# A hybrid decoder trunk on one core: adding the expert results during the last job, and level scores issued within a projection

## What is computed

```python
# HGRN2, per chunk: scores with a decay per feature
b = jnp.cumsum(gb, axis=2)
decay = jnp.exp(where(mask, b[:, :, :, None, :] - b[:, :, None, :, :], -inf))
scores = jnp.einsum('bhtd,bhsd,bhtsd->bhts', qb, kb, decay)
# experts: each token goes to its two best of 8, weighted by a softmax over the two
top_val, top_idx = lax.top_k(logits, TOP_K)
gates = jax.nn.softmax(top_val, axis=-1)
hid = jax.nn.silu(xb @ w_gate[e]) * (xb @ w_up[e])
ys = (hid @ w_down[e]) * gt[:, None]          # for the tokens of expert e
y = zeros.at[tok_pad].add(ys)                 # each token's two results are added
x = x + y
return rmsnorm(x, final_norm)
```

## Time and profile before

| | us |
|---|---|
| median of 3 runs | 1554.12 |
| lowest, highest | 1554.05, 1557.11 |
| the profiled execution, its own time | 1557.37 |
| its span, first to last instruction | 1555.6 |
| mean granted TensorE clock in it | 0.971 |

### The profile page before, as it was taken

One profiled execution on the slowest core, in us unless ns is written; L12 is line 12 of the kernel. 1 busy time (PEld: TensorE's weight loads), 2 busy tenths in 40 slices (PEclk: granted clock), 3 DMA queues, 4 the chain that ended last, 5 costly groups with the idle time before them and its releaser, 6 DMA issues.

```text
span 1555.6 us, 21085 instructions
## 1 busy us (share of the span) xinstructions
PE 1477.0 (95%) x8033; PEld 1257.2 (81%) x8033; DVE 1165.6 (75%) x921; ACT 952.6 (61%) x847; POOL 90.9 (6%) x103
## 2 busy tenths in 40 slices
PE   6999799997999979999999999999999999999993
PEld 6988499997988658888888888888888888888882
DVE  4883354544686258888888888888888888889884
ACT  4454244443545227777777777777777777777772
POOL 4221000000031120000000000000000000000001
PEclk8999999999899969999999999999999999999997
DMA  8431695543333169999999999999999999999983
GB/s 262 163 109 55 210 317 190 190 138 133 109 113 112 49 229 349 388 376 375 396 367 374 395 387 370 395 369 370 394 379 366 394 387 373 394 370 365 395 339 108
DMA packets 211785, 449.19 MB, mean 289 GB/s; under 512 B 12884, under 2 KB 37016, under 8 KB 211736
## 3 DMA queue, kind: packets, MB, share of 16 engines
q1 hardware_dynamic: 210584, 444.31, 78.5%
q0 software_dynamic: 1152, 4.19, 0.7%
HBM read 433.80 MB, written 14.68 MB: 288 GB/s over the span
## 4 chain that ended last, share of the span: by engine, by line
PE 89%; DVE 5%; ACT 2%; issue 1%; DMA 1%; SPq 1%; POOL 0%; DVEq 0%; POOLq 0%; ACTq 0%
PE bank L1371 26%; PE bank L1373 26%; PE bank L1372 26%; PE bank L1594 2%; PE bank L1581 2%; PE bank L1678 2%; ACT winh L711 1%; PE bank L1425 1%; DVE QD L995 1%; DVE low L1223 1%; DMA ring<-in_w_in_dram 1%; DVE winl L963 1%; DVE SC L1004 0%; ACT XN L679 0%; PE bank L1665 0%
## 5 line engine op out<-in xcount | busy, mean ns | idle before, releaser
L1223 DVE TENSOR_TENSOR low<-raw,high 128x2048 fp32r<-128x2048 f32 x336 | 769.1, 2298 | 112.2 <-ACT high L880 112.2
L880 ACT CAST high<-raw 128x2048 fp32r<-128x2048 f32 x336 | 644.6, 1919 | 178.0 <-PE bank L1373 178.0
L1371 PE MATMUL bank<-high,xeh 128*128 128x512 f32 x896 | 353.5, 395 | 0.0
L1373 PE MATMUL bank<-high,xel 128*128 128x512 f32 x896 | 349.5, 390 | 0.0
L1372 PE MATMUL bank<-low,xeh 128*128 128x512 f32 x896 | 348.8, 389 | 0.0
L1373 PEld LDWEIGHTS bank<-high,xel 128*128 128x128 f32 x896 | 168.2, 188 | 35.8
L1372 PEld LDWEIGHTS bank<-low,xeh 128*128 128x128 f32 x896 | 168.4, 188 | 33.7
L1371 PEld LDWEIGHTS bank<-high,xeh 128*128 128x128 f32 x896 | 168.3, 188 | 33.7 <-issue 0.2
L1371 PE MATMUL bank<-high,hdh 128*128 128x512 f32 x448 | 175.0, 391 | 0.0
L1373 PE MATMUL bank<-high,hdl 128*128 128x512 f32 x448 | 174.4, 389 | 0.0
L1372 PE MATMUL bank<-low,hdh 128*128 128x512 f32 x448 | 174.3, 389 | 0.0
(11 more groups left out here) (281 smaller groups left out, 1945.0 us busy)
## 6 DMA issues: line engine op xcount, KB each, us to landing
raw<-in_moe_w_gate_dram SPq DMA_DIRECT2D x112, 1024.0 KB, 7.7
raw<-in_moe_w_up_dram SPq DMA_DIRECT2D x112, 1024.0 KB, 8.2
raw<-in_moe_w_down_dram SPq DMA_DIRECT2D x112, 1024.0 KB, 7.7
ring<-in_w_in_dram SPq DMA_DIRECT2D x10, 2048.0 KB
dring<-in_dense_w_gate_dram SPq DMA_DIRECT2D x5, 2048.0 KB
dring<-in_dense_w_up_dram SPq DMA_DIRECT2D x5, 2048.0 KB
dring<-in_dense_w_down_dram SPq DMA_DIRECT2D x5, 2048.0 KB
ring<-in_w_in_dram SPq DMA_DIRECT2D x8, 1024.0 KB
```

The costliest lines, as they stand in the source:

```text
L880: act.copy(high[:, q % SPLIT, :], raw[:, q % RAW, :]).then_inc(s_hi, 1)
L1223: dve.tensor_tensor(low[:, q % SPLIT, :], raw[:, q % RAW, :], high[:, q % SPLIT, :].bitcast(F32), ALU.subtract).then_inc(s_lo, 1)
L1371: pe.matmul(o, xh, wh, start=first, stop=False)
L1373: return pe.matmul(o, xl, wh, start=False, stop=last)
```

## The change

In the layers, level k-1 is issued between the two groups of projection k+2, where level k stood behind projection k+2.

At the end:
- GpSimd prepares, behind the scatters of the tokens, selection matrices for the last job (picks: row = token, column = slot in the last job, value = the weight of that choice) and row numbers in which all places of the last job point to a block of `routed` that holds zeros (pick_last).
- At piece 16 of the last job (BACK_AT) VectorE converts these row numbers, and GpSimd gathers the results of all other jobs into a buffer of their own, multiplies each by its weight and adds it to X, while the last job runs.
- Behind the last job ScalarE and VectorE copy its results, TensorE turns the selection matrices (ScalarE copies them) and multiplies them with the results: four fp32 products of 128x128 by 128x512. VectorE adds these to X.
- Squares, scaling and stores go by halves of 512 features; mean and power by tiles.
- The last store to `routed` and the wait for it are gone.

```diff
+    BACK_AT = STORE_AT + 3
-        gathered = raw[:, :, :].rearrange("p r n -> p (r n)")[:, 0:2 * T * D]....
+        gathered = phase("experts", "gathered", [P, 2, T, D])
...
@@ SP
-            sp.wait_ge(s_yh, 2 * njobs + 2)
-            sp.dma_start(routed[bass.ds(njobs, 1), :, :]..., results[:, :]).then_inc(s_last, 16)
...
             for t in range(T):
-                sp.wait_ge(s_fin, t + 1)
-                sp.dma_start(out[0, t * P:(t + 1) * P, :], XN[:, t, :]).then_inc(s_out, 16)
+                for n in range(2):
+                    v = slice(n * BANK, (n + 1) * BANK)
+                    sp.wait_ge(s_fin, 2 * t + n + 1)
+                    sp.dma_start(out[0, t * P:(t + 1) * P, v], XN[:, t, v]).then_inc(s_out, 16)
@@ GpSimd
+            def pick_last():
+                first, rel, past, off = lastb[:, 0:1], lastr[:, 0, :, :], lastr[:, 1, :, :], lastr[:, 2, :, :]
+                step(pool.tensor_scalar(first, JB[:, 1, 15:16], float(P), None, ALU.mult))
+                step(pool.tensor_scalar(rel, places[:, :, :], first, None, ALU.subtract))
+                step(pool.tensor_scalar(past, rel, 0.0, None, ALU.is_ge))
+                step(pool.tensor_scalar(off, places[:, :, :], -1.0, float(P * (MAXJOBS + 1)), ALU.mult, ALU.add))
+                step(pool.tensor_tensor(off, off, past, ALU.mult))
+                step(pool.tensor_tensor(lastr[:, 3, :, :], off, places[:, :, :], ALU.add))
+                for t in range(T):
+                    for c in range(2):
+                        ins = pool.tensor_scalar(picks[:, c, t, :], iota[:, :], rel[:, c, t:t + 1], RV[:, 5 + c, t:t + 1],
+                                                 ALU.is_equal, ALU.mult)
+                step(ins)
+                for t in range(T):
+                    ins = pool.tensor_tensor(picks[:, 0, t, :], picks[:, 0, t, :], picks[:, 1, t, :], ALU.add)
+                ins.then_inc(s_pick, 1)
...
-            pool.wait_ge(s_last, 16)
+            pick_last()
+            pool.wait_ge(s_backi, 1)
             for t in range(T):
                 for c in range(2):
                     pool.indirect_dma_start(gathered[:, c, t, :], None, routed....,
-                                            bass.IndirectOffsetOnAxis(ap=placei[:, c, t:t + 1], axis=0))\
+                                            bass.IndirectOffsetOnAxis(ap=backi[:, c, t:t + 1], axis=0))\
                         .then_inc(s_back[t], 16)
-            inv_rms(2 * DEPTH)
+            for t in range(T):
+                pool.wait_ge(s_back[t], 32)
+                for c in range(2):
+                    g = gathered[:, c, t, :]
+                    pool.tensor_scalar(g, g, RV[:, 5 + c, t:t + 1], None, ALU.mult).then_inc(s_lb3, 1)
+                    pool.wait_ge(s_lb3, 2 * t + c + 1)
+                    if c:
+                        pool.wait_ge(s_ca, 2 * t + 1)
+                    pool.tensor_tensor(X[:, t, :], X[:, t, :], g, ALU.add).then_inc(s_ca, 1)
+            for t in range(T):
+                pool.wait_ge(s_ss, 2 * T * DEPTH + 2 * t + 2)
+                mean = st[:, 2 * DEPTH, 0, t:t + 1]
+                pool.tensor_scalar(mean, mean, fsq[:, t:t + 1], None, ALU.add).then_inc(s_fr, 1)
+                pool.wait_ge(s_fr, 3 * t + 1)
+                pool.tensor_scalar(mean, mean, 1.0 / D, EPS, ALU.mult, ALU.add).then_inc(s_fr, 1)
+                pool.wait_ge(s_fr, 3 * t + 2)
+                pool.tensor_tensor(st[:, 2 * DEPTH, 1, t:t + 1], mean, mhalf[:, 0:1], ALU.pow).then_inc(s_fr, 1)
@@ ScalarE
+            act.wait_ge(s_pickT, 1)
+            act.copy(pickT[:, :, :], ps[6][:, 0:T * P].rearrange("p (t s) -> p t s", t=T)).then_inc(s_pickc, 1)
             act.wait_ge(s_used, nth_use(last, NPC - 1))
-            for n in range(2):
-                results_out(last + 1, n)
+            act.copy(results[:, BANK:], ps[5][:, :]).then_inc(s_lres1, 1)
             square_sums(2 * DEPTH)
@@ VectorE
+            def add_last(t, n):
+                dve.wait_ge(s_lout, 2 * t + n + 1)
+                dve.wait_ge(s_ca, 2 * T)
+                xs = X[:, t, n * BANK:(n + 1) * BANK]
+                dve.tensor_tensor(xs, xs, ps[2 * t + n][:, :], ALU.add).then_inc(s_ca, 1)
+
+            def back_rows():
+                dve.wait_ge(s_lb2, 6)
+                dve.wait_ge(s_st, 16 * last + 32)
+                dve.tensor_copy(backi[:, :, :], lastr[:, 3, :, :]).then_inc(s_backi, 1)
...
+                    if is_last and q == BACK_AT:
+                        back_rows()
                     piece_low(j, q)
...
+            dve.wait_ge(s_used, nth_use(last, NPC - 1))
+            dve.tensor_copy(results[:, 0:BANK], ps[4][:, :]).then_inc(s_lres, 1)
             for t in range(T):
-                add_results(t)
+                for n in range(2):
+                    add_last(t, n)
...
@@ TensorE, layers
-                    project(l, k + 2, (lambda: attn_turn(l, k - 9, 1)) if k >= 9 else None)
+                    def between():
+                        if 1 <= k <= LEVELS:
+                            level(l, k - 1)
+                        if k >= 9:
+                            attn_turn(l, k - 9, 1)
+                    project(l, k + 2, between)
...
-                    if k < LEVELS:
-                        level(l, k)
@@ TensorE, end
+            pe.wait_ge(s_pick, 1)
+            for t in range(T):
+                ins = pe.transpose(ps[6][:, t * P:(t + 1) * P], picks[:, 0, t, :], ident[:, :])
+            ins.then_inc(s_pickT, 1)
+            pe.wait_ge(s_pickc, 1)
+            for t in range(T):
+                for n in range(2):
+                    pe.wait_ge(s_lres1 if n else s_lres, 1)
+                    pe.matmul(ps[2 * t + n][:, :], pickT[:, t, :], results[:, n * BANK:(n + 1) * BANK],
+                              start=True, stop=True).then_inc(s_lout, 1)
```

More of the change, by code:

```diff
@@ L234, in bass_hybrid_trunk_kernel @@
         first_slot = phase("experts", "first_slot", [P, T])
-        gathered = raw[:, :, :].rearrange("p r n -> p (r n)")[:, 0:2 * T * D].rearrange("p (c t d) -> p c t d", c=2, t=T)
+        gathered = phase("experts", "gathered", [P, 2, T, D])
+        picks = phase("experts", "picks", [P, 2, T, P])
+        pickT = phase("experts", "pickT", [P, T, P])
+        lastb = phase("experts", "lastb", [P, 2])
+        lastr = phase("experts", "lastr", [P, 4, 2, T])
+        backi = phase("experts", "backi", [P, 2, T], I32)
+        fsq = phase("experts", "fsq", [P, T])
         fgain = hT[:, 0:4, :].rearrange("p a b -> p (a b)")
@@ L357, in bass_hybrid_trunk_kernel @@
         s_st = sem("results_stored")
-        s_last = sem("last_results_stored")
+        s_lb2 = sem("last_job_steps")
+        s_pick = sem("last_job_picks")
+        s_backi = sem("gather_rows_ready")
+        s_pickT = sem("last_job_picks_turned")
+        s_pickc = sem("last_job_picks_copied")
+        s_lres = sem("last_results_copied")
+        s_lres1 = sem("last_results_upper_copied")
+        s_lout = sem("last_results_combined")
+        s_fr = sem("final_rms_steps")
+        s_lb3 = sem("weighted_results")
         s_back = [sem(f"results_gathered{t}") for t in range(T)]
@@ L537, in _ @@
                 job(j, e)
-            sp.wait_ge(s_yh, 2 * njobs + 2)
-            sp.dma_start(routed[bass.ds(njobs, 1), :, :].rearrange("o p d -> p (o d)"), results[:, :])\
-                .then_inc(s_last, 16)
             sp.wait_ge(s_lg, 1)
@@ L1308, in tokens_low, with final @@
                                       xeh[:, 4 * b:4 * b + 4, :].bitcast(F32), ALU.subtract).then_inc(s_xl, 1)
[L1310 to L1319, removed]
+            def add_last(t, n):
[7 more added lines that the diff above has]
+                dve.tensor_copy(backi[:, :, :], lastr[:, 3, :, :]).then_inc(s_backi, 1)
+            def final(t):
+                dve.wait_ge(s_fr, 3 * t + 3)
+                dve.wait_ge(s_fg, 16)
+                for n in range(2):
+                    v = slice(n * BANK, (n + 1) * BANK)
+                    dve.scalar_tensor_tensor(out=XN[:, t, v], in0=X[:, t, v], scalar=st[:, 2 * DEPTH, 1, t:t + 1],
+                                             in1=fgain[:, v], op0=ALU.mult, op1=ALU.mult).then_inc(s_fin, 1)
             def hidden_low(j, c):
@@ L1356, in _ @@
             job(last, is_last=True)
+            dve.wait_ge(s_used, nth_use(last, NPC - 1))
+            dve.tensor_copy(results[:, 0:BANK], ps[4][:, :]).then_inc(s_lres, 1)
             for t in range(T):
-                add_results(t)
-            dve.wait_ge(s_rms, 2 * DEPTH + 1)
-            dve.wait_ge(s_fg, 16)
+                for n in range(2):
+                    add_last(t, n)
             for t in range(T):
-                dve.scalar_tensor_tensor(out=XN[:, t, :], in0=X[:, t, :], scalar=st[:, 2 * DEPTH, 1, t:t + 1], in1=fgain,
-                                         op0=ALU.mult, op1=ALU.mult).then_inc(s_fin, 1)
+                final(t)
         @block.tensor
```

13 lines of the change are left out of this document (11 added, 2 removed).

## The result

The kernel after takes **1543.93 us** (median of 4 runs, 1543.34 to 1544.41) against 1554.13 (4 runs, 1554.05 to 1557.11) in the same series. These medians divide to 0.9934; the ratio on record is 0.9922, 95% interval 0.991 to 0.9933, so the gain is 10.2 us by the medians and 12 by the ratio. Forecast were 1544.4. The profiled execution of after took 1543.67 for a span of 1541.9.

The account below looks back on a forecast made before the run. TensorE, busy 95% of the span, was taken as the bound. Terms -12.0 - 4.6 - 1.4 + 8.3 = -9.7 gave 1547.7 us against the profiled execution, so a median of 1544.4; range 1540.5 to 1548, chance 0.58.

Parts of the forecast that it names:

- end: Behind the last matmul: the chain to the end of the span shrinks from 24.6 to 12.6 us, saving 12.0.
- levels: Both layers: seven TensorE waits on VectorE's copy go (-7.8 us), new waits add 3.2, net -4.6.
- clock: Projections partly at the lower TensorE clock: with fewer waits, one of two such stretches counted as gone, -1.4 us.
- additions under the last job: Last job: GpSimd's multiplications and additions delay VectorE's splits, giving +8.3 us of new TensorE waits.
- gathers and weights: Last job: gathers of 2.1 MB fit beside the weight stream, 5.5 us to spare; counted 0, high end 5.
- Rival C: Layers: the levels give nothing, as VectorE is the bound in some steps; 1549 us, chance 0.08.
- The port: Last job: GpSimd and VectorE take turns by whole instructions; GpSimd's eight operations hold the port 14.0 us.
- one lead of 1.0: Last job: splits are ready ahead of TensorE's need; 1.0 us of this cover taken off the 9.3 us lag.
- The low end of this term: Last job: GpSimd gets in only in VectorE's 0.4 us pauses, so only each addition's rest shows; 3.8 us.
- Rival A: Last job: the port costs little, up to 4 us; 1540 us, chance 0.17.
- Rival B: Last job: gathered rows make the weight stream late and TensorE waits 5 us more; 1549.5 us, chance 0.13.
- D: Last job: gathers hold the queues 18.3 us, weights behind them come late; slower than before, 1557.5 or more, chance 0.04.

Follow-up runs that it names:

- experiment 3: Only the levels moved, put into the kernel before the change: 1551.9 us (8 runs), ratio 0.9972.
- Experiment 1: The kernel before the change, run unchanged for a second profile: 1558.02 us (one run).
- experiment 4: The changed kernel with GpSimd's multiplications and additions made behind the last job, the gathers staying in it: 1557.84 us (one run).
- experiment 5: The changed kernel with GpSimd multiplying by the constant 0.5 in place of the weight column: 1546.13 us (one run).

## Why the prediction was right, and where it was not

| term | forecast | measured |
|---|---|---|
| end | -12.0 | -12.9 |
| levels | -4.6 | -4.8 by waits, -2.8 and -4.8 by medians |
| clock | -1.4 | -1.4 in the two stretches without levels, and no steady value |
| additions under the last job | +8.3 | +4.8 by profile, +5.1 by undoing |
| gathers and weights | 0 | 0 |

**The end** went as worked out: every step down to VectorE's last one is within 0.4 us of its forecast. Of the 0.9 us missed 0.7 are in the last term, "I keep it, since a half tile saves little of a landing": from VectorE's end it took 2.48 us instead of 3.2. GpSimd's steps beside the scaling of tile 0 were done 0.4 us before their forecast, so the 0.8 for the port was too much there as well.

**The levels**: all seven waits went, and the two per layer that should take their place came, 0.64 and 0.61 against 0.7, 1.06 and 1.07 against 0.9. Rival C (levels give nothing) is out: experiment 3 shows them faster alone. Here the method worked: move the step in the timeline, then ask of each engine what is late next.

**The clock** term was no forecast. Experiment 1 shows that its stretches move from execution to execution of one and the same kernel. Of the two in the earlier trace rows the second is gone in after, as forecast (clock 1.00 from 465 to 480), but it is gone in experiment 1 too, whose kernel is unchanged (1.00 from 468 to 480). The -1.4 measured lies in other stretches than the one forecast, so that the two numbers agree is chance.

**The port** is the step that failed: "So I take 1.2 for 1024 and 2.3 for an addition: 4 x 3.5 = 14.0 us of holding the port", and with it "Eight GpSimd operations alternate with eight splits". The additions were right (2.34 alone). The multiplication was wrong in three ways: it takes 2.86 alone, not 1.2; beside splits it takes 7.0, since it waits out two of them; and the split behind it is held up by 0.24 to 0.83 us only. So VectorE lost 9.05 us and not 14.0, on eight splits as the prediction had it, but with five others among them, over 38.8 us and not 31.7. The row behind the 1.2, is of an operation with constants and on another shape, and the other one there, on 128x8, was too small to show what a large one does.

What the lost time costs: VectorE pauses for 13.7 us in a job of 118, 11.6% of any stretch. Lost time minus these pauses is 9.05 - 0.116 x 38.8 = 4.5 us in after (the jobs grew by 4.8), 9 x (3.437 - 2.29) - 3.5 = 6.8 with the constant (7.3), and 9 x (3.819 - 2.29) - 3.9 = 9.9 with the two tiles (10.7). The prediction took off one lead of 1.0 instead. This bookkeeping orders the three kernels rightly and is 0.3, 0.5 and 0.8 us short of them; it was found after them and forecast in none.

The low end of this term, 3.8 (its own factors give 4 x 0.9 = 3.6), is nearer to the 4.8 measured than the 8.3 is, but its mechanism, GpSimd getting in only where VectorE pauses, is not what happened to the additions. The one at 1486.36 got in between two splits issued without a pause, and the second of them took twice its time:

```profile
1486.59 4.50 DVE L1286 TENSOR_TENSOR low<-raw,high 128x2048 fp32r<-128x2048 f32 x1
```

Rival A (port cheap, 1540) was half right, in its mechanism for the multiplications and not for the additions. Rival B (weights late) is out: landings rose to 14.0 us, inside the 15.4 that the prediction counted, and experiment 4 keeps the gathers without any wait. D fell with it.

The Trainium skill (SBUF — State Buffer, Who interferes with whom) has a VectorE instruction with two SBUF inputs contend with any GpSimd instruction that reads SBUF. The additions agree, with splits of up to 4.5 us. Of the one-input multiplication the trace agrees as far as GpSimd goes, which waited; VectorE lost much less than the 2.86 that a lock on the whole instruction would take. The same section's inference that descriptor generation leaves a tensor_tensor alone is borne out: the splits beside the four issues stayed at 2.29.

**The total** was right in part by luck. Against the profiled execution the steps said 1547.7, and 1543.67 came: 4.0 too much. The port term is 3.5 of it and the end 0.9; the layers with the clock gave 0.4 less than forecast (5.6 for 6.0). Against the median only 0.5 were missed, since the profile of before lay 3.25 above its own median: the forecast took these 3.25 us off in full, while they were partly time at the lower clock that the change was also credited with. And the 1554.12 from which it started was itself low: the later series of before have medians of 1555.44 to 1556.95. From these the kernel after is 11.5 to 13.0 us away, not the 9.7 of the sum.

## What to carry to other kernels

Work moved from a path's end onto an idle engine is free only if it doesn't take a port from the engine that feeds the bound; compare with doing it on the busier engine in its pauses, as one fused pass may cost less there than two elsewhere. Price an operation by a row of the same form (inputs, column or constant, size), and charge to the bound only the part that exceeds the pauses of the engine held up. Where work goes between two halves of a loop, walk through each engine's order once more: the two waits per layer that came could be had back by moving two instructions, and the one that stood behind them by one more.

## What the hardware did that was not expected

- GpSimd's multiplication of 128x1024 by a column takes 2.86 us alone and 7.0 beside the splits, where it waits for the split under way and the next one; with a constant 4.9, where it waits for the split under way only; as a product of two tiles 3.96. Why the column's version waits for two was not found out.
- Small operations of GpSimd wait as long as large ones. In the preparation one of 128x1, asked for 0.3 us behind the start of a split, took 2.12 us, and the split kept its 2.29; three of 128x4 behind it, ahead of the next split, took 0.2 to 0.3 each:

```profile
582.34 2.12 POOL L596 TENSOR_SCALAR lastb<-JB 128x1 f32<-128x1 f32 x1
```

- An indirect DMA takes GpSimd 2.14 to 2.85 us to issue in the last job, 0.94 to 0.98 at the old end, while the splits beside it keep their 2.29. Whether the splits or the full weight stream stretch it no run separates.
- An operation shorter by 2.1 us (experiment 5, one run) came with a kernel slower by 2.2 (and eight jobs longer by 2.5), as it packed the additions closer and held each split behind it up by more.
